# Half-size products for more of the two projections, with weight sums built in memory by DMA

## The reference

```
for l in range(2):
    h = rmsnorm(x, norm_gain[l])
    q, k, v, g_attn, x_rnn, g_rnn = split(h @ w_in[l])            # 2048 x 4352
    attn = sliding-window attention of q, k, v (chunks of 64, window 128, sinks, rotary positions)
    rnn  = gated linear recurrence over causal_conv(x_rnn)         # 64x64 gate products
    mixed = concat(attn * silu(g_attn), rnn * silu(g_rnn))         # 2048
    x = x + mixed @ w_out[l]                                       # 2048 x 2048
out = rmsnorm(x, final_gain)
```

## Time and profile before

| | us |
|---|---|
| median of 3 runs (lowest, highest) | 2312.78 (2311.39, 2314.31) |
| the profiled execution, its own time | 2313.38 |
| its span, first to last instruction | 2311.6 |
| PE busy | 2296.4 |
| DVE busy | 1637.6 |
| ACT busy | 1330.1 |
| DMA, mean over the span | 110 GB/s |

### The profile page before, as it was taken

The page is one execution under the profiler, slowest core; times in us unless marked ns, Lnnn a source line. Parts: engine busy times, 40 slices in busy tenths (PEclk is TensorE's granted clock), DMA queues, the critical chain, the costliest instruction groups (busy, mean ns, idle before and its releaser), DMA issues.

```text
span 2311.6 us, 36747 instructions
## 1 busy us (share of the span) xinstructions
PE 2296.4 (99%) x13690; PEld 1915.2 (83%) x13690; DVE 1637.6 (71%) x2767; ACT 1330.1 (58%) x2551; POOL 0.8 (0%) x10
## 2 busy tenths in 40 slices
PE   9999999999999999999999999999999999999999
PEld 8888888898888888888888888888888888888888
DVE  7568778766547877867675786787765478777775
ACT  7558666434456767644565676763354557666444
POOL 0000000000000000000000000000000000000000
PEclk9999999999999999999999999999999999999999
DMA  5334333434333233344435433233343333333344
GB/s 194 103 109 139 95 89 92 117 113 123 95 99 88 85 99 85 99 143 117 148 96 157 164 105 93 89 97 115 116 119 97 95 95 89 89 90 100 110 119 151
DMA packets 138563, 255.28 MB, mean 110 GB/s; under 512 B 15632, under 2 KB 30224, under 8 KB 137616
## 3 DMA queue, kind: packets, MB, share of 16 engines
q1 hardware_dynamic: 137808, 252.77, 36.6%
q10 hardware_dynamic: 576, 0.16, 0.0%
HBM read 244.48 MB, written 8.39 MB: 109 GB/s over the span
## 4 chain that ended last, share of the span: by engine, by line
PE 85%; DVE 8%; DMA 4%; issue 2%; ACT 2%; SPq 0%; DVEq 0%; ACTq 0%; POOL 0%; POOLq 0%
PE proj L508 75%; DMA wraw<-in_w 3%; PE proj L527 2%; DVE wcut L1140 2%; PE proj L541 2%; PE ps_at L621 1%; PE ps_at L646 1%; PE ps_at L665 1%; PE proj L557 1%; DVE x L1443 1%; ACT wcut L750 1%; DVE room L1154 1%; DVE wraw L1155 1%; DVE wraw L1156 1%; DVE room L1158 0%
## 5 line engine op out<-in xcount | busy, mean ns | idle before, releaser
L508 PE MATMUL proj<-operand,wcut 128*128 128x512 f32 x8520 | 1973.2, 391 | 0.3 <-DVE proj L1203 0.3
L508 PEld LDWEIGHTS proj<-operand,wcut 128*128 128x128 f32 x8520 | 1591.4, 188 | 343.9 <-issue 11.2
L750 ACT ACTIVATE wcut<-wraw 128x512 fp32r<-128x512 f32 x803 | 505.6, 630 | 768.4 <-PE proj L508 657.3
L1140 DVE TENSOR_TENSOR wcut<-wraw,wcut 128x512 fp32r<-128x512 f32 x804 | 553.6, 689 | 522.5 <-ACT wcut L750 517.7
L527 PE MATMUL proj<-xsum,wcut 128*128 128x256 f32 x720 | 99.4, 283 | 0.0
L527 PEld LDWEIGHTS proj<-xsum,wcut 128*128 128x128 f32 x720 | 92.1, 192 | 0.0
L907 ACT ACTIVATE room<-ps_at,stat 128x128 f32<-128x128 f32 x256 | 90.0, 363 | 0.8
L855 ACT ACTIVATE gy<-proj 32x512 f32<-32x512 f32 x144 | 85.0, 590 | 3.8
L760 ACT ACTIVATE crosscut<-room 128x384 fp32r<-128x384 f32 x80 | 42.0, 526 | 54.5 <-DMA room<-in_w 26.5
L541 PE MATMUL proj<-operand,crosscut 128*128 128x256 f32 x480 | 70.5, 283 | 0.0
L541 PEld LDWEIGHTS proj<-operand,crosscut 128*128 128x128 f32 x480 | 64.3, 192 | 1.2
(11 more groups left out here) (181 smaller groups left out, 1810.0 us busy)
## 6 DMA issues: line engine op xcount, KB each, us to landing
wraw<-in_w SPq DMA_DIRECT2D x804, 256.0 KB, 2.6
room<-in_w SPq DMA_DIRECT2D x80, 128.0 KB, 2.7
x<-in_xt SPq DMA_DIRECT2D x2, 4096.0 KB, 13.7
mixed<-in_xt SPq DMA_DIRECT2D x14, 512.0 KB, 7.1
gw<-in_gates SPq DMA_DIRECT2D x32, 128.0 KB, 2.7
out<-x SPq DMA_DIRECT2D x4, 1024.0 KB, 4.9
out<-mixed SPq DMA_DIRECT2D x7, 512.0 KB, 3.2
tab<-in_cossin SPq DMA_DIRECT2D x8, 256.0 KB, 3.5
```

Of the source, the lines that this page charges most:

```text
L508: last = pe.matmul(bank[:, :], wcut[:, u % RING, a, c:c + P], operand[:, k, b, :], start=(k == 0 and n == 0), stop=(k == KT - 1 and n == 2 ...
L750: act.activation(wcut[:, u % RING, 0, :], wraw[:, u % RING, :], ACT.Copy).then_inc(w_hi, 1)
L1140: dve.tensor_tensor(wcut[:, u % RING, 1, :], wraw[:, u % RING, :], wcut[:, u % RING, 0, :].bitcast(F32), ALU.subtract).then_inc(w_lo, 1)
```

## The change

The seven-product form is used in more groups. With h and l: input groups 6 to 15 in (0,0), 4 to 15 in (0,1), 7 to 15 in (1,0), 4 to 15 in (1,1), and output groups 19 to 24 (19 to 23 in the last stage): 43 groups of the input projection and 23 of the output projection, 66 in place of 20. In each, as before, half of the tiles k take the form.

The products are ordered in another way. A seven-product group has 4 plain units and 7 units of one block or block sum each (four `lead`, three `late`), each for four pairs of tiles at once: 12 matmuls of 256 tokens. So it has 11 units of weights to load and cut in place of 8. `BEAT` gives the units of a slot: none, one or two. In a group that is of the form and has a successor of the form the eight slots hold: late, late / plain / plain / late / lead, lead / lead, lead / plain / plain, the leads being the next group's. The cut of a slot's second unit stands at the end of the slot.

The weight sums are no longer made by DVE. POOL issues transfers from HBM to HBM: copies of a block into `sums`, and additions onto it (`accum_op`). They are for 34 groups (both layers), four sums each, in 17 batches of two groups, a chain of four transfers in each batch, begun when unit 8 is done. SP waits for a batch (`built`) before it loads a sum in the first half.

Token sums of the input projection take the place of `x`, from slots 24 to 30 (0,0), 6 to 11 (layer 1) or 25 to 49 (1,0) until group 15. So in layer 1 x is first stored to HBM (four transfers of 1 MB at slots 1 to 4), and in all four stages it is loaded back (4 MB) at slot 125, after the last product that uses the sums.

Evacuations move: the second tile of an xr group from six slots after the group to two, the q tiles from one every four slots to slots 0 and 2 of the next group.

```diff
+IN_FIRST = {(0, 0): 6, (0, 1): 4, (1, 0): 7, (1, 1): 4}
+IN_LAST = 15
+SEVEN = {(h, l): (*range(IN_FIRST[h, l], IN_LAST + 1),
+                  *range(PG + 2, PG + (7 if (h, l) == (LAST, DEPTH - 1) else 8)))
...
+    if mine and ahead:
+        return [t[:2], p[:1], p[1:2], t[2:], a[:2], a[2:], p[2:3], p[3:]]
+    if mine:
+        return [t[:1], t[1:2], p[:1], t[2:], p[1:2], [], p[2:3], p[3:]]
+    if ahead:
+        return [p[:1], p[1:2], p[2:3], [p[3], a[0]], [p[4], a[1]], [p[5], a[2]], a[3:], p[6:]]
...
-Q_EV = 16
+Q_AT = [2 * UPG + UPG * (t // 2) + 2 * (t % 2) for t in range(AT)]
-XR_EV = [slot_of("xr", j) + 6 * (j % 2) for j in range(RT)]
+XR_EV = [slot_of("xr", j) + 2 * (j % 2) for j in range(RT)]
+RELOAD = UPG * IN_LAST + 5
...
+                            if h == 0 and what in SUMS:
+                                sp_.wait_ge(built[what], 32 * (batch_of(UNIT[next_u][1], g) + 1))
+                            sp_.dma_start(wraw[:, u % RING, :], source(next_u)).then_inc(w_in[u % RING], 16)
...
+                        if s == RELOAD:
+                            sp_.wait_ge(unit_done, TURNED[h, l, "in"])
+                            if l == 0:
+                                sp_.dma_start(x[:, :, :], xt[h]).then_inc(xres_in, 16)
+                            else:
+                                sp_.dma_start(x[:, :, :].rearrange("p (i k) t -> p i (k t)", i=4),
+                                              x_kept.rearrange("i p c -> p i c")).then_inc(xres_in, 16)
...
+            pool.wait_ge(unit_done, START_SUMS)
+            for n in range(len(BATCH) + 1):
+                now, before = n < len(BATCH), n > 0
+                if before:
+                    copy(S4, n - 1, S2)
+                if now:
+                    copy(S1, n, A21)
+                    copy(S3, n, A11)
+                    pool.wait_ge(built[S1], 32 * n + 16)
+                    add(S1, n, A22)
+                    pool.wait_ge(built[S3], 32 * n + 16)
+                    add(S3, n, A21)
...
+                    copy(S2, n, S3)
+                    pool.wait_ge(built[S2], 32 * n + 16)
+                    add(S2, n, A22)
...
+                        if (i, p) == (NPAIR - 1, 2):
+                            next_bank(n + 1)
                         last = pe.matmul(bank_of(l, 2 * g + m)[:, HT * half:HT * half + HT],
+                                         wcut[:, n % RING, a, P * i:P * i + P], src,
+                                         start=(kind == "lead" and j % 2 == 0 and (i, p) == (0, 0)),
...
-            def weight_sums(h, l, g, i):
-            def cross_cut_lo(h, l, g, i):
...
+            def lead_half_sum(h, l, g):
+
+                n = LED.index((h, l, g))
+                dve.wait_ge(lead_copy, n + 1)
+                dve.tensor_tensor(lead_u[:, :], lead_u[:, :], bank_of(l, 2 * g)[:, HT:TOK], ALU.subtract).then_inc(lead_half, 1)
...
+                dve.tensor_tensor(first[:, HT:TOK], second[:, HT:TOK], lead_u[:, :], ALU.add).then_inc(lead_done, 1)
+                dve.tensor_tensor(lead_v[:, :], second[:, 0:HT], lead_u[:, :], ALU.subtract).then_inc(lead_done, 1)
+                dve.wait_ge(lead_done, 3 * n + 2)
+                dve.tensor_tensor(second[:, HT:TOK], lead_v[:, :], second[:, HT:TOK], ALU.subtract).then_inc(lead_done, 1)
```

More of the change, by code:

```diff
@@ new lines, with zone_of, beats_of @@
+NPAIR = 4
+JS = {"in": (0, 1, 4, 5), "out": (0, 1, 2, 3)}
+LEAD = ((0, 0, 0, None), (1, 0, 1, 1), (3, 1, 1, 0), (2, 1, 0, 2))
+LATE_OF = ((4, 0, 0, None), (5, 0, 1, None), (6, 1, 0, 3))
+A11, S2, S3, S1, A12, S4, A22, A21 = range(8)
+WHOLE = {A11: 0, A12: 1, A21: 2, A22: 3}
+SUMS = {S1: 0, S3: 1, S2: 2, S4: 3}
+def zone_of(g):
+    return "in" if g < PG else "out"
+def beats_of(h, l, g):
+    mine, ahead = g in SEVEN[h, l], g + 1 in SEVEN[h, l]
+    p = [("plain", g, j) for j in range(UPG) if not mine or j not in JS[zone_of(g)]]
+    a = [("lead", g + 1, b) for b in range(4)]
+    t = [("late", g, b) for b in range(3)]
+    if mine and ahead:
[4 more added lines that the diff above has]
+        return [p[:1], p[1:2], p[2:3], [p[3], a[0]], [p[4], a[1]], [p[5], a[2]], a[3:], p[6:]]
+    return [[n] for n in p]
@@ new lines, in sums_at, with tiles_read, after @@
+def sums_at(h, l, g):
+    return UPG * (g - 1) + (6 if g - 1 in SEVEN[h, l] else 7)
+def tiles_read(kind, g, j):
+    if kind == "plain":
+        return {KU * j, KU * j + 1}
+    if (kind, j) == ("lead", 0):
+        return {KU * i for i in JS[zone_of(g)]}
+    return {KU * i + 1 for i in JS[zone_of(g)]} if kind == "late" and j < 2 else set()
+def after(test):
+    return 1 + max(n for n, unit in enumerate(UNIT) if test(*unit))
+READ = {(h, l, zone, k): after(lambda *u: u[:2] == (h, l) and zone_of(u[3]) == zone and k in tiles_read(*u[2:]))
+        for h in range(HALVES) for l in range(DEPTH) for zone in JS for k in range(KT)}
@@ new lines @@
+OWN = {(h, l, g): after(lambda *u: u[:2] == (h, l) and u[3] == g and u[2] != "lead")
+       for h in range(HALVES) for l in range(DEPTH) for g in range(PG + OG)}
+LED = [(h, l, g) for h in range(HALVES) for l in range(DEPTH) for g in SEVEN[h, l]]
+LED_AT = [[after(lambda *u: u == (h, l, "lead", g, b)) for h, l, g in LED] for b in range(4)]
+ZONES = [(h, l, zone) for h in range(HALVES) for l in range(DEPTH) for zone in JS
+         if any(zone_of(g) == zone for g in SEVEN[h, l])]
+TURNED = {at: after(lambda *u: u[:2] == at[:2] and zone_of(u[3]) == at[2] and u[2] != "plain") for at in ZONES}
@@ L163, in build @@
         x = sb("x", [KT, TOK])
+        x_end = nc.sbuf_base
         mixed = sb("mixed", [KT, TOK])
@@ L343, in at_sq, with at_t, source, batch_of @@
             return h * (3 * KT) - max(h - 1, 0) * X_EARLY + n - (X_EARLY if h else 0)
[L345 to L355, removed]
+        def at_t(h, l, zone, n):
+            return NPAIR * ZONES.index((h, l, zone)) + n + 1
+        def source(n):
+            h, l, kind, g, j = UNIT[n]
+            if kind == "plain":
+                return w[l, g, j]
+            what = (LEAD if kind == "lead" else LATE_OF)[j][0]
+            if what in WHOLE:
+                return blocks[WHOLE[what], l, g].rearrange("r (q c) -> (r q) c", c=TOK)
+            return sums[SUMS[what], l, g].rearrange("r (q c) -> (r q) c", c=TOK)
+        def batch_of(l, g):
+            return next(n for n, (bl, first, size) in enumerate(BATCH) if bl == l and g - first in range(size))
         def bank_of(l, tile):
@@ L402, in _ @@
                     for s in range(SLOTS):
[L403 to L410, removed]
+                        for u in BEAT[h, l, s]:
+                            next_u = u + RING if u + RING < TOTAL else u + RING - UPG
+                            kind, g, j = UNIT[next_u][2:]
+                            what = {"lead": LEAD, "late": LATE_OF}[kind][j][0] if kind != "plain" else None
+                            sp_.wait_ge(w_lo, u + 1)
+                            if h == 0 and what in SUMS:
+                                sp_.wait_ge(built[what], 32 * (batch_of(UNIT[next_u][1], g) + 1))
+                            sp_.dma_start(wraw[:, u % RING, :], source(next_u)).then_inc(w_in[u % RING], 16)
```

492 lines of the change are left out of this document (262 added, 230 removed).

## The result

The changed kernel takes 2430.98 us (median of 4 runs, 2429.3 to 2432.09), against 2313.55 of the kernel before (4 runs): ratio 1.0508, 95% interval 1.0495 to 1.0521. The forecast was 2294, and faster.

A forecast was written before the change was run, and what follows sets the result against it. PE, busy 2296.4 of 2311.6 us, was taken to bound the kernel: 2313.4 - 34.8 (cheaper products) - 7.5 (residual wait gone) + 6.8 (busiest stretches) + 10 (load of x) + 6 (evacuation) = 2293.9, about 2294 us; range 2270 to 2321.

The forecast's parts named there:

- PE's gain: Seven-product groups: half-size matmuls at 119.8 ns save 0.76 us a group, 34.8 us over 46 more groups.
- Evacuation ahead of the leads: Leads of groups 5 and 6 in layer 1 wait for a q tile turned in slot 3: 4 x 1.5 = 6 us.
- My bound of 30 us: Upper bound on lead waits for evacuation, if each of 43 input leads waits half of 1.4 to 1.5 us.
- The busiest stretches: Attention, recurrence and gates together: DVE needs 86.1 us, PE 84.4, so PE waits 1.7 us per stage, 6.8 in all.
- my upper bound, 25 us: Busiest stretch of each stage: if waits for ACT leave DVE 95% busy, PE loses 6.2 us per stage, 25 in all.
- DVE and ACT block each other: Rival, chance 0.16: in busy stretches runs of small units shrink the lead over PE; 18 us more, 2312, no change.
- The load of x: Slot 125: weights queue behind the 4 MB load, ready near 16.0 us, so PE waits 2.5 us four times: 10 us.
- The sums by DMA: HBM-to-HBM batches take 20 to 28 us each and arrive in time; nothing taken for lateness.
- loads slowed by the sums: Rival, chance 0.15: until 360 or 500 us sums slow weight landings to 5.6 us; costs 12 to 37 us, about 2319.
- The stores of x: Layer 1: four 1 MB stores, one a slot, end before the first token sums; costed at nothing, uncovered some 3 us.
- the arithmetic's 2271: Whole kernel, rival with chance 0.20: ring of four absorbs the added waits, so 2313.4 - 42.3 = 2271 us.

The follow-up runs named there:

- the output-only kernel with the late start: Changed kernel with the seven-product form only in output groups, x loaded at slot 60, POOL's sums started after unit 72 instead of 8: 2305.61 us, ratio 0.9966.
- the pieces: Changed kernel with the 4 MB load of x cut into eight 0.5 MB transfers, one every second slot from slot 125: 2410.3 us, ratio 1.0414.
- the three causes: Changed kernel with unsummed blocks loaded instead of POOL's sums, leads waiting only for their own bank, and x loaded in eight transfers: 2323.45 us, ratio 1.0045.

## Why the prediction was wrong

**PE's gain: right.** 24 half-size matmuls of the input projection start in 2.87 us (731.09 to 733.96 us), 119.6 ns each, against the 119.8 from the earlier trace rows. In the output projection the leads no longer wait for the residual, and the output-only kernel with the late start shows that gain by itself: 7.7 us where 9.8 was the sum; 3.2 us of waits at the turn of stages stay. The Trainium skill's sustained figures in TensorE: Matmul & The Clock Gate, Back-to-back issue gap, were rightly left out of the sum.

**"Evacuation ahead of the leads", 6 us: one of the two steps that failed most.** The experiments give 50.3 alone and 39.1 behind the pieces. I counted one mechanism, a q tile in slot 3 with its shifts already done, in two groups of layer 1. At these four places the places were right and the size was not: waits of 3.2 and 6.0 us in each of the two stages, 18.4 in all, since ACT's shifts had themselves waited for DVE's tile before, and the cut stood behind them. The other 54.5 us of such waits are at xr and gate groups and at the last plain unit ahead of the form, at which I took none. The traces of two of them show what stands ahead: at the q tile a cut that waits for ACT, at the gate other work of a DVE that is busy throughout PE's wait. For the other places the cause is argued from these two. My bound of 30 us, half of 1.4 us in each of 43 leads, was too small: the waits sum to 73 us.

**"The busiest stretches", 6.8 us.** Halving DVE's cut gives 25.6 where ACT's gives 0.9, so DVE's work in the input groups costs at least that, more than the term. The work was sized right (DVE 1769 us for 1766). The failed step is to ask of it only that it fit into the time: 86 us in 84. DVE makes PE wait at 94% already. That my upper bound, 25 us, comes so near is luck: it was for four busy stretches, and the cuts were halved in all input groups. In the changed kernel itself the sign that I named, DVE over 95% busy from 174 to 261 us, did not come: it was busy in 61.2 of 87 us, 70%, because other waits had slowed PE first. Of the rivals, *DVE and ACT block each other* is what the q tile shows in kind.

**"The load of x", 10 us.** The mechanism is right: PE stops 13.6 to 13.9 us after each of the four issues, as said. The waits are 15.8 us in sum for 10, with 18.7 us to the first weights in stage 1 in place of 14.6 and two or three waits behind a load where I had one; cutting up the load gave 20.7.

**"The sums by DMA", nothing: the other step that failed most.** Lateness was rightly left out: SP shows no wait for `built`, and the last transfer is issued at 532 us, some 30 us a batch, a little over the 20 to 28. What was costed at nothing was their traffic; I had it as a rival, *loads slowed by the sums*, at 12 to 37 us and 0.15. It is worth 37.5 alone and 47.8 with the others mended, landings of 4.7 to 7.5 us for the 5.6 that the earlier trace rows gave.

**The clock: no term at all.** 42.3 us of the 117.2 are put down to PE's work at the lower clock. The earlier trace rows show a full clock, and I read that as a constant of the kernel; it held while PE hardly waited. Every wait was priced at its own length, and in this kernel 110 us of waits cost 152. The Trainium skill, TensorE: Matmul & The Clock Gate, What's actually happening, says that the gate goes to 1.2 GHz after PE was idle and returns to 2.4 GHz after it was busy; the trace agrees (0.56 to 0.59 after a wait of 4.7 us, and 1.00 again behind that), and the rule would have told against the range.

**"The stores of x"** I take as right at nothing: in the first 60 us of stages 2 and 4 PE waits once in each, 1.4 us, and for DVE's x (L1567). It was not tried alone.

**What the parts leave.** 2431.0, less 107.5 for the three causes, less 25.6 for DVE's cuts, is 2297.8; the arithmetic's 2271 lies 27 us lower. That rest I did not take apart: 18.4 us of it are PE's waits that DVE still makes, 9.7 for the cut of weights, 5.1 for the evacuation of q and 3.6 for the attention's operands (xcut), and halving is not removing. That these waits go with DVE's remaining work was not tried.

## What to carry to other kernels

Before work is added beside a full PE, list for each wait of PE what stands ahead of its releaser in that engine's order, not only how long the releaser takes; and halve the lead in time when the units get half as long. Read how busy an engine is by stretches of a few groups: here PE waited for DVE where it was 92 to 94% busy, and did not at 82 to 85%. Price PE's waits with the clock behind them, here 1.4 times their length in sum, and put heavy background traffic beside long units and away from large loads.

## What was unexpected of the hardware

- A POOL transfer of 512 KB between HBM buffers landed in 5.5 us as a copy and in 7.7 us as an addition (medians, 3.9 to 8.8 and 5.3 to 13.7), in the same traffic; an addition took 1.4 times as long as a copy of the same size.
- With them running, all 16 DMA engines were 80 to 97% busy at only 209 to 314 GB/s, where the first 29 us of the kernel before moved 296 GB/s at 82%.
- Weight loads that landed in 4.3 us in place of 2.6, beside such traffic, cost PE nothing while it had plain units to multiply.
